# A two-block transformer layer on one NeuronCore: clearing of the gates later, the queries' second rope behind the first, the root for their scale behind the last splits

## The reference

```python
def mla_group(q_lat, kv_lat, k_pe, positions, q_a_gain, w_q_b, ...):
    q = (rms_norm(q_lat, q_a_gain) @ w_q_b).reshape(B, S, MLA_HEADS, MLA_QK)   # 8 heads of 128 + 64
    ...
    q = rms_norm(q, q_gain)
    q = jnp.concatenate([q[..., :MLA_NOPE], rope(q[..., MLA_NOPE:], positions)], axis=-1)
    k = jnp.concatenate([k[..., :MLA_NOPE], rope(k[..., MLA_NOPE:], positions)], axis=-1)
    ...
    s = jnp.einsum('bqhd,bkhd->bhqk', qb, k) * scale
```

## Time and profile before

| | |
|---|---|
| time, median of 3 runs | 3259.15 us (3258.58 to 3262.24) |
| the profiled execution | 3259.14 us |
| its span in the trace | 3257.3 us |
| PE busy | 3200.2 us, 98% of the span |
| DVE, ACT, POOL busy | 2106.2, 1517.7, 492.0 us |

### The profile page before, as it was taken

The page is one execution under the profiler, slowest core; times in us unless marked ns, Lnnn a source line. Parts: engine busy times, 40 slices in busy tenths (PEclk is TensorE's granted clock), DMA queues, the critical chain, the costliest instruction groups (busy, mean ns, idle before and its releaser), DMA issues.

```text
span 3257.3 us, 40800 instructions
## 1 busy us (share of the span) xinstructions
PE 3200.2 (98%) x16112; PEld 2715.7 (83%) x16112; DVE 2106.2 (65%) x3062; ACT 1517.7 (47%) x2006; POOL 492.0 (15%) x322
## 2 busy tenths in 40 slices
PE   8989999999999999999999999999999999999998
PEld 7788888888888888888888888888888788888886
DVE  6766578887555576666666565565465655655556
ACT  5645454545444444444444544445444544444443
POOL 1000005777777200000000000000000000000000
PEclk9999999999999999999999999999999999999999
DMA  8623557888888866666665555444555455555554
GB/s 321 252 85 130 181 183 208 214 214 215 212 214 211 262 249 244 250 248 245 245 233 200 197 184 174 165 170 176 191 194 188 174 192 191 193 189 193 189 192 149
DMA packets 220286, 660.95 MB, mean 203 GB/s; under 512 B 56704, under 2 KB 56848, under 8 KB 217536
## 3 DMA queue, kind: packets, MB, share of 16 engines
q1 hardware_dynamic: 170864, 600.81, 52.9%
q0 software_dynamic: 49232, 57.54, 8.7%
HBM read 622.48 MB, written 35.78 MB: 202 GB/s over the span
## 4 chain that ended last, share of the span: by engine, by line
PE 90%; DVE 6%; ACT 2%; issue 1%; DMA 1%; DVEq 0%; ACTq 0%; SPq 0%
PE PS L1649 89%; DVE wlo L2102 2%; PE PS L1723 2%; ACT whi L1872 1%; DMA raw<-in_w_in_b 0%; DVE R L2606 0%; ACT M L1914 0%; DVE AA L2148 0%; ACT Y L1958 0%; DVE TMP L2177 0%; DVE M L2507 0%; DVE TMP L2178 0%; DVE BB L2148 0%; DMA R<-in_x 0%; DMA M<-in_na_bias 0%
## 5 line engine op out<-in xcount | busy, mean ns | idle before, releaser
L2102 DVE TENSOR_TENSOR wlo<-raw,whi 128x1024 fp32r<-128x1024 f32 x1101 | 1343.8, 1224 | 889.6 <-ACT whi L1872 878.4
L1872 ACT ACTIVATE whi<-raw 128x1024 fp32r<-128x1024 f32 x1101 | 1157.8, 1057 | 1033.4 <-PE PS L1649 998.3
L1649 PE MATMUL PS<-whi,AA 128*128 128x512 f32 (+1 forms) x2880 | 718.7, 390 | 2.0 <-DVE AA L2148 1.2
L1649 PE MATMUL PS<-whi,BB 128*128 128x512 f32 x2640 | 667.4, 393 | 1.7 <-DVE wlo L2102 1.2
L1649 PEld LDWEIGHTS PS<-whi,AA 128*128 128x128 f32 x2880 | 537.0, 189 | 112.4 <-DVE AA L2148 2.0
L1649 PE MATMUL PS<-BB,whi 128*128 128x512 f32 x2304 | 577.4, 392 | 1.7 <-DVE BB L2148 1.7
L1649 PEld LDWEIGHTS PS<-whi,BB 128*128 128x128 f32 x2640 | 491.1, 188 | 102.3 <-DVE wlo L2102 1.8
L2699 POOL DMA_INDIRECT scr_g<-M x256 | 446.9, 1746 | 426.4 <-issue 390.2
L1649 PEld LDWEIGHTS PS<-BB,whi 128*128 128x128 f32 x2304 | 414.4, 189 | 76.1 <-DVE BB L2148 1.9
L1649 PE MATMUL PS<-wlo,AA 128*128 128x512 f32 (+1 forms) x1440 | 389.4, 388 | 1.9 <-DVE wlo L2102 1.9
L1649 PE MATMUL PS<-wlo,BB 128*128 128x512 f32 x1320 | 356.3, 389 | 0.5 <-DVE wlo L2102 0.5
(11 more groups left out here) (236 smaller groups left out, 1570.0 us busy)
## 6 DMA issues: line engine op xcount, KB each, us to landing
raw<-in_peer_u SPq DMA_DIRECT2D x256, 512.0 KB
raw<-in_peer_v SPq DMA_DIRECT2D x256, 512.0 KB
raw<-in_w_in SPq DMA_DIRECT2D x160, 512.0 KB
raw<-in_w_up SPq DMA_DIRECT2D x128, 512.0 KB
raw<-in_w_down SPq DMA_DIRECT2D x128, 512.0 KB
raw<-in_w_out SPq DMA_DIRECT2D x64, 512.0 KB
raw<-in_w_in_a SPq DMA_DIRECT2D x32, 512.0 KB
scr_g<-M POOLq DMA_DIRECT2D x8, 2048.0 KB, 30.1
```

Of the source, the lines that this page charges most:

```text
L1649: return e.matmul(outp, l, r, start=start, stop=stop)
L1872: e.activation(whi[:, n % NH, :], raw[:, n % NR, :], ACT.Copy).then_inc(s_hi, 1)
L2102: e.tensor_tensor(wlo[:, n % NH, :], raw[:, n % NR, :], bf(whi[:, n % NH, :]), ALU.subtract).then_inc(s_lo, 1)
```

## The change

Three things. `gate_blank` is given PE's latest mark, the end of the last product of `queries(1)`, so that the strip and the eight clearing DMAs start behind it. `q_rope` makes both squares, then both gains, then both ropes with no `yield` between them. `q_scale` waits until the six splits of the queries are in the program.

```diff
             def q_rope(ts, te, j):
-                tr = []
+                xs, ta, tr = [heads(ts[:, t, :], 8) for t in range(2)], [], []
                 for t in range(2):
-                    x = heads(ts[:, t, :], 8)
-                    a = yield from squares(x, 8, ssq[:, 1, t, :], te)
-                    t_ssq.append(a)
-                    go("gain_rows", x, gq, 8, fresh("DVE", a, t_gr))
-                    a = up("DVE", "gained")
-                    yield
-                    tr.append(rope(ts[:, t, :].rearrange("p (u c h) -> p u c h", u=8, c=2), 8, 32, CS[:, 0, t], CS[:, 1, t],
-                                   [a, t_rope, x_read], Y[:, 0, 1024:2048]))
-                    yield
+                    ta.append((yield from squares(xs[t], 8, ssq[:, 1, t, :], te)))
+                t_ssq.extend(ta)
+                for t in range(2):
+                    go("gain_rows", xs[t], gq, 8, fresh("DVE", ta[t], t_gr))
+                    tr.append(up("DVE", "gained"))
+                for t in range(2):
+                    tr[t] = rope(ts[:, t, :].rearrange("p (u c h) -> p u c h", u=8, c=2), 8, 32, CS[:, 0, t], CS[:, 1, t],
+                                 [tr[t], t_rope, x_read], Y[:, 0, 1024:2048])
+                yield
                 while not a_free:
                     yield
...
             def q_scale():
-                while len(t_ssq) < 6:
-                    yield
-                yield
+                while len(t_ssq) < 6 or len(qt_done) < 6:
+                    yield
                 go("q_scale", ssq, rq, fresh("DVE", t_ssq, latest["DVE"]))
...
-            go("gate_blank")
+            go("gate_blank", fresh("POOL", latest["PE"]))
             t_blank = up("POOL", "gate_blank")
...
-            def gate_blank():
+            def gate_blank(ready):
+                for mark in ready:
+                    e.wait_ge(*mark)
                 e.memset(blank, 0.0).then_inc(sem("gate_blank"), 1)
```

## The result

The changed kernel takes 3308.75 us (median of 5 runs, 3307.86 to 3310.28) against 3258.58 us in the same runs: slower by 1.54% (ratio 1.0154, 95% interval 1.0139 to 1.0169), 50 us. The profiled execution's span is 3307.9 us, 50.6 longer than before.

A forecast was written before the change was run, and what follows sets the result against it. PE was taken as the bound, busy 3200.2 of 3257.3 us. Scores 45.1 us later, less 2.7 for clock and 0.6 for early relief, gave +41.8: 3301 us, range 3293 to 3313, with room down to 3286.

The forecast's parts named there:

- the hold of POOL: POOL's queue: the eighth clear is issued only once the seventh has landed, at 202.5, so the second zeroing ends at 204.6.
- the clears alone ran at another rate than beside loads: Sign that the forecast is wrong; it had expected DMA near 415 GB/s for 35 us during the clears.
- The stall behind the ropes: PE, free at 139.9 in the projections, stands until both ropes are done at 148.0: 8.1 us.
- The size of the transfer: Seven clears, 14.68 MB, have all of DMA at 415 GB/s: 35.4 us, landing at 202.0.
- Early relief: Clears no longer share DMA with loads of 40 to 117 us, so PE waits less for weights: -0.6 us, bounds 0 and -3.8.
- The tail: From PE resuming after the second spread of the keys to the first scores: 6.7 us instead of 10.0.
- Clock at the scores: First MLA scores run at full clock instead of half clock for 5.4 us: -2.7 us, bounds -2.7 and 0.
- the clock behind the stall: PE works at half clock for 5.4 us after resuming from its wait for the ropes, losing 2.7 us.
- POOL is not held: Rival, 7 in 100: all eight clears are issued in about 9.2 us, zeroing ends at 172.8; +10 us, 3269.
- the zeroing is not late: Rival, 5 in 100: the second zeroing ends before DVE needs it at about 164; +1 us, 3260.
- the edits win what they aim at: Rival, 2 in 100: transposes do not hold PE at 139.9 and the path loses 8.2 us; 3251.

The follow-up runs named there:

- the clearing alone: Kernel before with only the first edit, the strip and clears waiting for PE's last product: 3305.33 us, ratio 1.0144.

## Why the prediction was right

It held in direction, range and main mechanism, the hold of POOL: 3301 forecast, 3286 to 3313 given, 3308.75 measured. That the number came so near is in part luck, since errors of both signs cancel. One of the prediction's own signs of being wrong came true: the clears alone ran at another rate than beside loads. By its own steps:

- *The stall behind the ropes.* 8.1 us forecast, 8.00 in the profile, with the releaser that I had named. PE resumed at 144.91 and was at half clock until 147.8, for 2.9 us instead of the 5.4 that I took: the clock had fallen 3.8 us before PE resumed. The term of 2.7 us was 1.5 (1.11 and 3.12 us for what takes 0.66 and 2.09 at full clock).
- *The hold.* The eighth clear began 49.85 us after the first (forecast: 39.9), half a microsecond behind the seventh's landing. That the hold moves with the clears is shown by the clearing alone, and that it is in the eighth's issue by the kernel with the zeroing ahead of it.
- *The size of the transfer.* This is the term that was mis-sized. I took seven clears at 415 GB/s, a rate of a stretch in which loads ran beside them; alone they ran at 336 (343 from SP's queue), and first issue to seventh landing was 49.3 us instead of 39.4. The 10 us are more than the whole error of the sum, 7.8. The eighth clear came after 41.86 us of standing, not 32. The rate of the Trainium skill, page "DMA: Bandwidth & Descriptors", section "Anatomy of one DMA", 436 GB/s, is further from it still.
- *Early relief.* -0.6 forecast, -3.0 measured (the same four transposes at 139.25 before, 136.25 after), of which 0.3 was there ahead of the first clear (POOL's first zeroing at 37.54 and 37.23). My reason, late weights, was wrong: 2.3 us of the 3.0 are there at 50 us already, and the kernel with the clears behind the angles gets all of it while the clears still share DMA with the loads. The wait that goes is the 1.86 us one, the longest of the five that I had read; I had allowed that a DVE task could have made it, but had not asked what slowed DVE.
- *The tail.* 6.7 us from PE's resumption to the scores forecast, 7.2 measured, against 10.0 before.
- *Clock at the scores.* The granted clock is 1.00 from 216.2, and the scores start at 217.64, as forecast. They start 50.64 us late, and by the eight transposes of `Y` behind the attention PE is only 48.37 late (208.70 before, 257.07 after), so 2.3 us of the 2.7 are won. Then 1.6 us of them are lost in one stretch, in which PE is at half clock after and at full clock before. Before:

```profile
208.70 1.04 PE L1723 MATMUL PS<-C,Y 128*128 128x128 f32 x8
...
210.98 1.07 PE L1649 MATMUL PS<-whi,AA 128*128 128x512 f32 x4
...
230.50:237.20 6.70, 5.47 (x19) 4.89 (x20) 6.31 (x27) 2.40 (x10) 0.00 (x0) 0.50 0.24 90
```

and after:

```profile
257.07 1.88 PE L1722 MATMUL PS<-C,Y 128*128 128x128 f32 x8
...
260.96 1.07 PE L1648 MATMUL PS<-whi,AA 128*128 128x512 f32 x4
...
255.00:260.40 5.40, 5.17 (x28) 4.84 (x29) 4.85 (x11) 2.25 (x5) 0.00 (x0) 0.70 0.00 0
281.10:287.70 6.60, 5.99 (x20) 5.26 (x21) 6.05 (x25) 2.29 (x10) 0.00 (x0) 0.50 0.24 80
```

The stretch at half clock from 281.1 has its like before, from 230.5, and costs only 0.3 us more than that; the one that shows as 0.70 has none. Why the clock falls there stays open: just ahead of it PE waited for 0.34 and 0.55 us, against 0.34 and 0.39 at the same place before.

The sum: the last product 6.3 us later instead of 11.4, PE's resumption after it 47.1 us more than before instead of 37.0 (53.45 against 6.38), the tail 2.8 less instead of 3.3, which are the 50.6 at the scores instead of 45.1. At the end of the profiled executions it is 50.6 again, so nothing was left of the -2.7 for the clock. Against the forecast of 41.8, that is +10.1 in the transfer, +2.7 in the clock at the scores and +0.5 in the tail, against -2.4 in relief (-3.0 and not -0.6), -1.2 in the clock behind the stall and some -0.8 in the stall and the products behind it: 8.8 us between the profiled executions, and 7.8 between forecast and median.

Of the rivals, "POOL is not held" fell with the 41.86 us row, and "the zeroing is not late" with it; "the edits win what they aim at" fell with the 8.00 us row.

## What to carry to other kernels

A step that is moved in a queue takes along everything behind it: look at what stands next in the same engine's program and who waits for it, not only at the moved step. An idle stretch that cost nothing where it was (57 us of POOL, before anyone needed it) is a debt that falls due when it is moved. And a bandwidth taken from a stretch with reads and writes together says little about one of them alone.

## What the runs showed of the hardware

- POOL's issue of a DMA can stand for tens of microseconds with no semaphore in it: once 14,336 elements of 1 KB (seven DMAs of 2048) or 15,360 (fifteen of 1024) were issued, the next that would make 16,384 stood for 41 to 58 us, until 0.4 to 0.6 us after the last of them had landed. The first of them had landed 30 us and more earlier and had freed nothing. The Trainium skill, page "Perfetto Trace Analysis", section "DMA Instruction — SWDGE (GPSIMD)", says that engines may start on a DMA's descriptors before its issue ends when more are made than fit in the buffer; the rows fit a buffer that fills, but show a wait until all that was issued is through.
- These writes to HBM (1 KB elements from one strip), with no loads beside them, ran at 331 to 343 GB/s from two different queues; in the changed kernel the first 4 us were at 404. With loads beside them the sum was 415. The Trainium skill, page "HBM Reference", section "Specifications (TRN2)", gives about 358 GB/s for each of two cores that stream together, and about 425 for one that streams alone; here the program ran on one core, which reached 415 with loads and writes together, while its writes by themselves stayed below both figures.
- While POOL issues DMAs, small DVE instructions on SBUF (`TENSOR_SCALAR` of 128x64 float32) took 1.12 and 3.77 us instead of 0.20, one after the other, while a `TENSOR_TENSOR` of 128x1024 stayed at 1.23. The Trainium skill, page "SBUF — State Buffer", section "Who interferes with whom", states that DVE and GpSimd share a pair of ports under an exclusive lock, which `tensor_scalar` and `cast` can take in some modes and `tensor_tensor` needs only for reads; these rows agree in which operation is slow and which is not. Which port was held no run here shows.
